# A gated recurrence inside a decoder layer: chunks of 32 tokens against chunks of 64, with operands laid by head and token

## The chip, the cores and the metric

One core of one Trainium2 chip runs the whole program. The metric is device time in microseconds (us) of one execution; the kernel before has a median of 2337.99 us over 3 runs (2333.99 to 2338.67). Engines are called as in the profile: PE (TensorE matmuls), PEld (its weight loads), DVE (VectorE), ACT (ScalarE), POOL (GpSimd), SP (SyncE, which only issues transfers).

## The reference

One layer on x of 2048 tokens by 1024, float32: a norm, an input projection, a token mixer, an output projection, a residual, and then a gated MLP with a convolution. The change concerns the token mixer's recurrence, 8 heads of 64:

```python
def step(state, inp):                       # one token, per head
    r_t, w_t, k_t, v_t, a_t, b_t = inp
    sa = jnp.einsum('bhvk,bhk->bhv', state, a_t)
    state = (state * w_t[:, :, None, :] + sa[..., None] * b_t[:, :, None, :]
             + v_t[..., None] * k_t[:, :, None, :])
    y_t = jnp.einsum('bhvk,bhk->bhv', state, r_t)
    return state, y_t
...
y = rwkv7_recurrence(r_h, hs(decay), k_mod, v_h, -kk, kk * alpha_h)
mean = jnp.mean(y, axis=-1, keepdims=True)
var = jnp.mean(jnp.square(y - mean), axis=-1, keepdims=True)
y = (y - mean) * lax.rsqrt(var + GN_EPS) * ln_x_w + ln_x_b      # by head
return (y + bonus) * g
```

Both kernels compute it in chunks: within a chunk the tokens act on one another through a triangular matrix made of products of b and a, whose inverse is applied to what comes from the state and from v (giving u), and the state then takes b times u plus k times v. The inverses of 32 by 32 blocks are found on DVE, row by row.

## The kernel before

Three parts follow one another. `phase_project` (0 to about 541 us) does the norm and the input projection in 4 blocks of 512 tokens, makes r, k, v, a, b and the decays, and stores them to DRAM. `phase_recur` (548 to about 860 us) runs the recurrence. `mix_out_programs` and `phase_out_and_ffn` do the rest. In the projection and the MLP nearly every product is split in three (`split_matmul`, L133 to L135).

In `phase_project` the names that matter are `rows` (it turns a block of features by tokens into tokens by features on PE, L899), called for v and for a (`dec`), and `a_rows`, `store_rows` and `store`, with which ACT copies and stores them; `gram` (L915) makes the products of b and a of which DVE later inverts the 32 by 32 blocks (`solve` for blocks 0 and 1 of the sequence, in this phase).

`phase_recur` works on tiles of SC = 128 tokens, N = 16 of them, in a software pipeline. `iterations` calls `body(i)` for i from -2 to 19 on each engine. `stages(i)` says what runs: a1 (loads and grams of tile i+2), a2 (preparation of tile i+1), b (state steps of tile i), o (output of tile i-1), c (group norm of tile i-2), d (turning and gating of tile i-3). Every engine has its own program, in the order written, and waits on semaphores with constants. In one steady body PE does, with fp32 operands:

- b: four times, once for each 32-token chunk, `from_state` (4 products, L1673) and `to_state` (8 products, L1681); between them ACT reads u (`read_u`, L1402), and after them DVE updates the state (`advance`, L1553, or L1556 and L1559).
- a2: `bk_transposes` (16 turns of 128x128, L1706), `z0_products` (16, L1729), `w_products` (32, L1747), `z` (16, L1666).
- a1: `grams` (32, L1717), masked by DVE in two instructions (`masks`, L1565).
- o: `from_r` (32, L1694) and `from_uv` (32, L1702). d: the turning of y (4, L1781).

That is 228 products, of which 20 are turns. DVE also does the group norm (L1592 to L1627, six instructions, with the square on ACT) and, in `gap`, the rows of the inverses of blocks 2 and 3 (L1500, L1509, L1511: 27 parts per block, 8 gaps in a body). POOL copies b and k into the zero-padded layout `bk` (L1353, 8 copies in a body) and applies bonus and gate (L1367, L1369). SP issues 18 loads in a body: b, k, a, r, v (4), a by rows (4), the inverses (4, `spread`), bonus and gate.

## Time and profile before

| | |
|---|---|
| median of 3 runs | 2337.99 us |
| span of the profiled execution | 2329.1 us |
| PE busy | 2231.0 us (96%) |
| PEld, DVE, ACT, POOL busy | 78%, 75%, 49%, 44% |
| PE records / weight loads | 16652 / 16652 |
| DMA | 395.6 MB, mean 170 GB/s |

The profiled execution's span goes from its first to its last instruction; no other time of that same execution is given, and the median of the runs is 8.9 us longer than the span. Matmuls are pipelined and their ends are modelled: a PE that reads as busy may be waiting between two starts. So in the stretches of small products the starts and the counts of the records are read here, not the busy time. A plain fp32 product is two MATMUL records and two LDWEIGHTS records; a turn (transpose) is one of each.

### The profile page before, as it was taken

The page shows a single profiled execution, that of the slowest core. Times are in us where ns is not written, and L with a number is a line of the kernel's source. Part 1 is how long each engine was busy: PE and PEld are TensorE (multiplying, and loading weights), DVE is VectorE, ACT ScalarE, POOL GpSimd, SP SyncE. Part 2 cuts the span into 40 slices and gives each one's busy share as a digit, 9 for nine tenths or more (in the row PEclk, how much of TensorE's full clock was granted, in tenths as well). Part 3 has the DMA queues.
Part 4 walks back from the last instruction along what each step waited for, and adds up shares of the span by engine and source line. Part 5 has one row for each costly group of instructions (what it writes and reads, how often), then busy time and mean ns, then how long its engine had stood idle before and what let it go on. Part 6 is the DMA issues. An engine that isn't in the chain of part 4 may idle for free.

```text
span 2329.1 us, 43634 instructions
## 1 busy us (share of the span) xinstructions
PE 2231.0 (96%) x16652; PEld 1816.6 (78%) x16652; DVE 1756.5 (75%) x1910; ACT 1141.8 (49%) x1795; POOL 1025.4 (44%) x726
## 2 busy tenths in 40 slices
PE   7999999996999979998999999999999999999998
PEld 6777777775878768887888888788788888887886
DVE  3756798994884466769989999666799898976565
ACT  5646556452445554444444444454554444444543
POOL 4636466571234335535776766100146555541000
PEclk9999999998999989999999999999999999999999
DMA  7364556347567547895434343677733332326774
GB/s 203 93 227 134 178 160 209 106 140 216 154 166 194 144 144 234 268 279 166 153 119 147 121 146 128 217 252 255 237 119 115 104 111 93 113 95 202 247 260 145
DMA packets 435819, 395.61 MB, mean 170 GB/s; under 512 B 59548, under 2 KB 352076, under 8 KB 432332
## 3 DMA queue, kind: packets, MB, share of 16 engines
q1 hardware_dynamic: 407804, 343.06, 47.8%
q10 hardware_dynamic: 27856, 50.34, 6.0%
q8 instruction: 111, 1.82, 0.3%
q14 instruction: 48, 0.39, 0.1%
HBM read 266.97 MB, written 126.35 MB: 169 GB/s over the span
## 4 chain that ended last, share of the span: by engine, by line
PE 55%; DVE 3%; DMA 2%; ACT 1%; issue 1%; SPq 0%; ACTq 0%; POOLq 0%; POOL 0%; DVEq 0%
PE late_bank L133 18%; PE late_bank L134 18%; PE late_bank L135 18%; DVE wt_lo L2906 1%; DMA scratch_a<-p_keep 1%; ACT wt_hi L2727 1%; PE late_bank L2199 1%; DMA o_lo<-scratch_q 0%; DVE wt_lo L2860 0%; DMA p_keep<-in_w_down 0%; DMA raw<-in_w_down 0%; DMA scratch_x<-x_tile 0%; DMA p_keep<-scratch_td 0%; DVE p_ub L2869 0%; DVE x_tile L2168 0%
## 5 line engine op out<-in xcount | busy, mean ns | idle before, releaser
L133 PE MATMUL late_bank<-o_hi,wt_hi 128*128 128x512 f32 x1232 | 481.3, 391 | 8.0 <-DVE o_lo L2962 3.3
L134 PE MATMUL late_bank<-o_lo,wt_hi 128*128 128x512 f32 x1232 | 480.7, 390 | 0.0
L135 PE MATMUL late_bank<-o_hi,wt_lo 128*128 128x512 f32 x1232 | 480.6, 390 | 0.0
L431 POOL TENSOR_TENSOR p_w_lo<-p_w_raw,p_w_hi 128x1024 fp32r<-128x1024 f32 x72 | 190.4, 2645 | 221.2 <-ACT p_w_hi L502 221.2
L133 PEld LDWEIGHTS late_bank<-o_hi,wt_hi 128*128 128x128 f32 x1232 | 232.0, 188 | 58.7 <-issue 7.2
L135 PEld LDWEIGHTS late_bank<-o_hi,wt_lo 128*128 128x128 f32 x1232 | 232.1, 188 | 48.8
L134 PEld LDWEIGHTS late_bank<-o_lo,wt_hi 128*128 128x128 f32 x1232 | 232.0, 188 | 47.8
L2597 POOL TENSOR_TENSOR tsum<-raw 128x512 f32<-128x512 f32 x43 | 106.2, 2469 | 358.5 <-DVE p_ub L2947 179.4
L133 PE MATMUL p_ppr<-p_hT_hi,p_w_hi 128*128 128x512 f32 x576 | 233.4, 405 | 0.2 <-ACT p_ring L513 0.2
L133 PE MATMUL late_bank<-wt_hi 128*128 128x512 f32 x572 | 223.2, 390 | 7.2 <-DVE wt_lo L2906 6.6
L135 PE MATMUL p_ppr<-p_hT_hi,p_w_lo 128*128 128x512 f32 x576 | 226.6, 393 | 0.0
L134 PE MATMUL p_ppr<-p_hT_lo,p_w_hi 128*128 128x512 f32 x576 | 226.5, 393 | 0.0
L135 PE MATMUL late_bank<-wt_hi,wt_lo 128*128 128x512 f32 x572 | 222.6, 389 | 0.0
L134 PE MATMUL late_bank<-wt_lo,wt_hi 128*128 128x512 f32 x572 | 222.6, 389 | 0.0
L2674 ACT ACTIVATE wt_hi<-tsum 128x512 fp32r<-128x512 f32 x172 | 107.4, 627 | 169.3 <-PE late_bank L135 165.2
L2906 DVE TENSOR_TENSOR wt_lo<-raw,wt_hi 128x1024 fp32r<-128x1024 f32 x96 | 121.3, 1265 | 90.9 <-ACT wt_hi L2727 90.5
L2869 DVE TENSOR_TENSOR p_ub<-late_bank,p_ub 128x512 f32<-128x512 f32 x220 | 150.2, 683 | 34.6 <-PE late_bank L135 33.3
L2860 DVE TENSOR_TENSOR wt_lo<-raw,wt_hi 128x512 fp32r<-128x512 f32 x130 | 153.5, 1181 | 28.8 <-ACT wt_hi L2674 28.7
L2727 ACT ACTIVATE wt_hi<-raw 128x1024 fp32r<-128x1024 f32 x96 | 101.6, 1061 | 116.0 <-PE late_bank L135 96.9
L2860 DVE TENSOR_TENSOR wt_lo<-tsum,wt_hi 128x512 fp32r<-128x512 f32 x173 | 153.3, 887 | 1.8 <-ACT wt_hi L2674 0.6
L133 PEld LDWEIGHTS p_ppr<-p_hT_hi,p_w_hi 128*128 128x128 f32 x576 | 109.2, 190 | 36.3 <-issue 12.7
L133 PEld LDWEIGHTS late_bank<-wt_hi 128*128 128x128 f32 x572 | 107.4, 188 | 32.4 <-issue 6.4
(328 smaller groups left out, 4679.3 us busy)
## 6 DMA issues: line engine op xcount, KB each, us to landing
raw<-in_w_up SPq DMA_DIRECT2D x88, 512.0 KB, 5.1
p_w_raw<-in_w_in SPq DMA_DIRECT2D x72, 512.0 KB, 3.9
scratch_a<-p_keep SPq DMA_DIRECT2D x22, 1280.0 KB, 4.5
raw<-scratch_a SPq DMA_DIRECT2D x96, 256.0 KB, 3.0
raw<-scratch_td SPq DMA_DIRECT2D x52, 256.0 KB, 3.7
p_keep<-scratch_a SPq DMA_DIRECT2D x47, 256.0 KB, 2.9
scratch_a<-p_keep SPq DMA_DIRECT2D x44, 256.0 KB, 2.0
raw<-in_w_down SPq DMA_DIRECT2D x44, 256.0 KB, 4.1
```

The source lines that it names most:

```text
L133: nc.tensor.matmul(out, lhs_hi, rhs_hi, start=start, stop=False, skip_group_check=again)
L134: nc.tensor.matmul(out, lhs_hi, rhs_lo, start=False, stop=False, skip_group_check=again)
L135: return nc.tensor.matmul(out, lhs_lo, rhs_hi, start=False, stop=stop, skip_group_check=again)
L431: nc.gpsimd.tensor_tensor(w_lo[i][:, :, :], w_raw[i][:, :, :], w_hi[i][:, :, :].bitcast(F32), ALU.subtract).then_inc(s_wl, 1)
L2199: last = nc.tensor.transpose(bank[:, 4 + 2 * p + k // 4, (k % 4) * P:(k % 4 + 1) * P], hx[p][:, k * P:(k + 1) * P], ident[:, :])
L2597: nc.gpsimd.tensor_tensor(T1, B12, B11, ALU.subtract).then_inc(s_t, 1)
L2674: nc.scalar.activation(wt_hi[:, ph, :, :], weights(p, ph), ACT.Copy).then_inc(s_uh, 1)
L2727: nc.scalar.activation(dn_hi[r], dn_raw[r], ACT.Copy).then_inc(s_dh, 1)
L2860: nc.vector.tensor_tensor(wt_lo[:, ph, :, :], weights(p, ph), wt_hi[:, ph, :, :].bitcast(F32), ALU.subtract).then_inc(s_ul, 1)
L2869: nc.vector.tensor_tensor(dst, bank[:, b, :], src, ALU.add).then_inc(s_cd, 1)
L2906: nc.vector.tensor_tensor(dn_lo[r], dn_raw[r], dn_hi[r].bitcast(F32), ALU.subtract).then_inc(s_dl, 1)
```

## The change

The recurrence now works on chunks of L = 64 tokens. The tile of 128 tokens has two chunks and eight heads, and all operands lie with head h of a pair on partitions 64h to 64h+63, or with the tokens of a chunk there. A product takes 64 partitions and gives 64; `half(h)` to `half(h)` or `half(h)` to `other(h)`. In most loops two kinds of product alternate, so that four successive products name the four different 64x64 corners of the array:

```diff
+                    def from_state(c2):
+                        pe.wait_ge(s_z, ONE + i + 1)
...
+                        for j in range(PAIRS):
+                            for h in range(2):
+                                own = nc.tensor.matmul(pbank[half(h), c2 * PAIRS + j, :], ar[now][half(h), j, 0, tokens(c2)],
+                                                       st[p][c2][half(h), j, :], start=False, stop=True, skip_group_check=True)
+                                kv = nc.tensor.matmul(sbank[half(h), j, :], bkt[p][other(h), 1, (c2 * PAIRS + j) * H:(c2 * PAIRS + j + 1) * H],
+                                                      uv[now][other(h), 1, c2 * PAIRS + j, :], start=j == 0, stop=False, skip_group_check=True)
...
+                    def inverse(j, h, c2):
+                        u = c2 * PAIRS + j
+                        return nc.tensor.matmul(ubank[half(h), u, :], xt[now][half(h), j * 2 + c2, :], pz[half(h), u, :],
+                                                start=True, stop=True, skip_group_check=True)
```

The PE body before and after, in the order of the program (the number of products of the body after is in the table below):

```diff
-                        from_state(0)
...
-                        bk_transposes(0)
...
-                        to_state(0)
...
-                        from_r(0)
...
+                    if b:
+                        from_state(0)
+                    if o or a2:
+                        from_r_and_gram_of_a()
+                    if b or o:
+                        inverse_first()
+                    if a2:
+                        corner()
+                    if d:
+                        turn_y()
+                    if b or o:
+                        to_state_first()
+                    if o:
+                        from_u()
+                    if b:
+                        from_state(1)
+                    if a2:
+                        corner_right()
+                    if b or a2:
+                        inverse_second()
+                    if a2:
+                        gram_of_b_and_turn_k()
+                    if b or a2:
+                        to_state_second()
+                    if a2:
+                        turn_b_and_z()
+                        corner_left(0)
+                        corner_left(1)
```

| loop after | products | kinds, corners |
|---|---|---|
| from_state (0), (1) | 2 x 16 | state times a, and k times v: four corners |
| from_r_and_gram_of_a | 32 | r times state, and a with k: four |
| inverse_first, to_state_first | 2 x 16 | inverse or b times u, and v into y: four |
| inverse_second, to_state_second | 2 x 16 | inverse or b times u, and r with k: four |
| gram_of_b_and_turn_k, turn_b_and_z | 2 x 32 | r with b and turned k; turned b and z: four |
| turn_y, from_u | 2 x 16 | one kind: two corners |
| corner, corner_right, corner_left (0), (1) | 16, 16, 8, 8 | 32 wide: they make the lower block of the 64x64 inverse from the two 32x32 ones |

The sum is 272. Turning is done with plain products by the identity, no longer with `transpose`. `corner_left(1)` waits for `corner_left(0)` to be complete. The other engines:

```diff
-                        act.wait_ge(s_p1, ONE + i * CH + c4 + 1)
-                        nc.scalar.activation(uv[slot - 1][urows(e), c4, :, :], ubank[p][urows(e), c4 // 2, :, :], ACT.Copy).then_inc(s_u, 1)
...
+                        act.wait_ge(s_as, ONE + i * 2 + c2 + 1)
+                        nc.scalar.activation(pz[:, four(c2), :], pbank[:, four(c2), :], ACT.Copy).then_inc(s_p, 1)
...
+                        act.wait_ge(s_xp, ONE + i * 2 + c2 + 1)
+                        nc.scalar.activation(uv[i % BATCH][:, 0, four(c2), :], ubank[:, four(c2), :], ACT.Copy).then_inc(s_u, 1)
...
+                GAPS = 6
+                TURNS = 5
...
+                        nc.gpsimd.tensor_tensor(y[n % 3][:, :, :], y[n % 3][:, :, :], stat[p][:, 0, :].unsqueeze(2).to_broadcast([P, HEADS, H]),
+                                                ALU.add).then_inc(s_yc, 1)
...
+                        nc.gpsimd.tensor_tensor(y2[:, :, :], y[n % 3][:, :, :], y[n % 3][:, :, :], ALU.mult).then_inc(s_sq, 1)
...
+                        nc.gpsimd.tensor_tensor(y[n % 3][:, :, :], y[n % 3][:, :, :], stat[p][:, 3, :].unsqueeze(2).to_broadcast([P, HEADS, H]),
+                                                ALU.mult).then_inc(s_yc2, 1)
```

POOL no longer copies b and k; it takes over centring, squaring and scaling of y (three instructions of 128x512), and keeps bonus and gate. DVE masks three grams of 128x512 instead of two of 128x1024, updates the state twice with two instructions each instead of four times with one or two, and gets a 32x32 block transpose of 128x128. The rows of the inverses are spread over 5 bodies of 6 gaps. ACT reads p and u twice each, l21, m1, turned k, turned b, y and the corner x21.

In `phase_project` `a_rows`, its turns on PE and its stores go; the stores of a, r, b, k, bonus and gate go to arrays laid (block, partition, pair, tile, kind, token) in pieces of 128 tokens. SP loads two kinds in one transfer: b with k, a with r, bonus with gate; v in 2 transfers; the inverses in 12 (4 into `xt`, 8 into `xd`). That is 17 loads in a body. At the start of the recurrence the five parameter loads are the first of SP, and body -2 has no PE work.

## Rows read from the trace of the kernel before

**Rows 1.** Busy time of the page, and of bodies 0 to 14 of the recurrence (PE, PEld, DVE, ACT, POOL, clock, DMA share, GB/s).

```profile
PE 2231.0 (96%) x16652; PEld 1816.6 (78%) x16652; DVE 1756.5 (75%) x1910; ACT 1141.8 (49%) x1795; POOL 1025.4 (44%) x726
...
579.99:814.18 234.19, 220.10 (x6100) 190.24 (x6096) 156.19 (x306) 117.07 (x270) 78.14 (x132) 0.99 0.60 165
```

**Rows 2.** Timeline of PE in one body: start, us, line, product, records.

```profile
617.04 0.68 PE L1673 MATMUL late_bank<-p_st,p_w 128*64 128x64 f32 x8
617.65 0.66 PE L1706 MATMUL late_bank<-p_ident,first_bk 128*128 128x128 f32 x4
618.24 0.69 PE L1681 MATMUL late_bank<-p_uv,p_bkt 128*64 128x64 f32 x16
618.85 0.65 PE L1694 MATMUL late_bank<-p_st,p_ar 64*32 64x64 f32 x32
619.43 0.66 PE L1781 MATMUL late_bank<-p_ident,p_y 128*128 128x128 f32 x4
...
621.21 0.69 PE L1681 MATMUL late_bank<-p_uv,p_bkt 128*64 128x64 f32 x16
...
625.84 1.15 PE L1729 MATMUL late_bank<-p_uv,am 64*64 64x64 f32 x32
...
632.46 0.68 PE L1673 MATMUL late_bank<-p_st,w 128*64 128x64 f32 x8
```

**Rows 3.** Groups of PE: products of 512 columns on 64 and on 128 rows; turns of a.

```profile
L892 PE MATMUL p_pm<-p_um,p_wlora 64*128 64x512 f32 x64 | 15.9, 615 | 0.0
L884 PE MATMUL p_pm<-p_um,p_wgate 128*128 128x512 f32 x32 | 14.4, 592 | 0.0
...
L899 PE MATMUL p_pm<-p_ident,p_dec 128*128 128x128 f32 x48 | 5.7, 272 | 0.0
```

**Rows 4.** Windows between starts after stalls, columns as in the second of rows 1.

```profile
781.15:804.70 23.55, 21.66 (x635) 18.96 (x635) 10.38 (x19) 11.98 (x28) 5.54 (x10) 1.00 0.52 148
...
698.20:703.05 4.85, 3.88 (x126) 3.48 (x127) 1.66 (x4) 3.11 (x8) 2.54 (x2) 1.00 1.00 287
717.46:721.45 3.99, 3.73 (x137) 3.41 (x129) 2.88 (x5) 1.51 (x4) 3.41 (x8) 1.00 0.60 163
...
801.01:804.70 3.69, 3.49 (x136) 3.18 (x133) 2.34 (x5) 2.00 (x5) 0.00 (x0) 1.00 0.22 66
```

**Rows 5.** DMA queues from 781.1 to 804.7 us and from 580 to 815 us.

```profile
q8 instruction: 5, 0.08, 1.2%
...
q8 instruction: 48, 0.79, 1.4%
```

**Rows 6.** PE starts after idle time with no releaser; then such waits in the projection.

```profile
703.07 1.39 PE L1717 MATMUL late_bank<-ar,bk 128*64 128x64 f32 x40 [0.95 <-issue]
...
PE p_pm L915 <- issue: 8.5, 4, 2.8
```

**Rows 7.** Timelines of ACT and DVE in that body: reading u, updating the state.

```profile
617.76 0.38 ACT L1402 ACTIVATE p_uv<-late_bank 64x256 f32<-64x256 f32 x1 [1.22 <-PE late_bank L1673]
...
622.01 0.42 DVE L1556 TENSOR_TENSOR p_sumst<-late_bank,p_st 128x256 f32<-128x256 f32 x1 [0.39 <-PE late_bank L1681]
622.48 0.43 DVE L1559 TENSOR_TENSOR p_st<-p_sumst,chunk_decay 128x256 f32<-128x256 f32 x1
622.93 0.69 DVE L1592 TENSOR_REDUCE p_stat<-p_y 128x8 f32<-128x512 f32 x1
```

**Rows 8.** Groups of DVE in the recurrence: rows of the inverses.

```profile
L1511 DVE TENSOR_TENSOR p_inv<-p_inv,p_prod 128x30 f32<-128x30 f32 (+14 forms) x60 | 25.1, 419 | 2.1
L1509 DVE TENSOR_TENSOR p_prod<-p_inv 128x30 f32<-128x30 f32 (+14 forms) x60 | 23.7, 396 | 0.9
```

**Rows 9.** Timelines of DVE and of POOL at the same moment.

```profile
624.97 0.19 DVE L1509 TENSOR_TENSOR p_prod<-p_inv 128x30 f32<-128x30 f32 x1
625.20 1.30 DVE L1511 TENSOR_TENSOR p_inv<-p_inv,p_prod 128x30 f32<-128x30 f32 x1
...
625.17 1.28 POOL L1367 TENSOR_TENSOR p_mo<-p_mo,p_bonus 128x512 f32<-128x512 f32 x1 [11.96 <-DMA p_gate<-scratch_g]
```

**Rows 10.** Window with the clock at half, and PE's timeline there.

```profile
642.30:649.10 6.80, 6.80 (x119) 6.06 (x119) 3.91 (x6) 3.35 (x8) 3.81 (x6) 0.50 0.81 229
...
643.96 1.08 PE L1694 MATMUL late_bank<-p_st,p_ar 64*32 64x64 f32 x32
```

**Rows 11.** Timelines: ACT at the projection's end, PE at the recurrence's start and end.

```profile
542.43 1.27 ACT L556 ACTIVATE p_gate<-p_pm,p_par 128x512 f32<-128x512 f32 x2 [0.44 <-ACT p_cum L595]
...
557.18 1.11 PE L1706 MATMUL late_bank<-p_ident,first_bk 128*128 128x128 f32 x4 [4.01 <-DMA p_lnb<-in_ln_x_b]
...
819.83 0.68 PE L1673 MATMUL late_bank<-p_st,p_w 128*64 128x64 f32 x8 [0.57 <-ACT p_w L1392]
...
832.13 1.08 PE L1694 MATMUL late_bank<-p_st,p_ar 64*32 64x64 f32 x32 [0.86 <-ACT p_y L1472]
```

More of the change, by code:

```diff
@@ L37 @@
 CH = SC // C
+L = 2 * C
+HEADS = 2 * PAIRS
 UNITS = PAIRS * CH
@@ L652, in _ @@
                             high_w(n + WB)
-                        if f == 1 and b > 0:
-                            a_rows(b - 1, [pm[:, g, :] for g in range(TT)])
                         if f == 2:
@@ L929, in small @@
                 def small(b, pair):
-                    if pair == 0 and b > 0:
-                        pe.wait_ge(s_abr, ONE + b)
-                        rows(dec, [pm[:, g, :] for g in range(TT)], s_atn)
                     if pair in (2, 3) and b > 0:
@@ L1188, in job @@
             for other in JOBS[:JOBS.index(name)]:
-                if TURN[other] == t and (d if other[0] == "y" else a2):
+                if TURN[other] == t and (d if other == "y" else a2):
                     before += 1
@@ L1284, in body @@
+                        for h in range(2):
+                            sp.dma_start(uv[n % BATCH][other(h), 1, :, :].rearrange("s (c j) v -> s c (j v)", c=2), vrow[n, h]).then_inc(s_v[n % 2], 16)
+                        if n == 1:
+                            load_ab(FIRST)
+                            sp.dma_start(above[:, :, :], const_view(a, "above")).then_inc(s_ab, 16)
                     if N - 2 - KT <= i < N - 2:
@@ L1473, in body @@
                     if a2:
[L1474 to L1480 removed]
+                        take("x21", *((xt[(i + 1) % BATCH][quad(h, 0), :, C:L].rearrange("s (j c) t -> s c j t", c=2),
+                                       lambda v, h=h: v[quad(h, 0), 0:HEADS * C].rearrange("p (c j t) -> p c j t", c=2, t=C)) for h in range(2)))
@@ new lines, in to_state, with r_of_k @@
+                    def to_state(j, h, c2):
+                        u = c2 * PAIRS + j
+                        return nc.tensor.matmul(sbank[half(h), j, :], bkt[p][half(h), 0, u * H:(u + 1) * H], uv[now][half(h), 0, u, :],
+                                                start=False, stop=True, skip_group_check=True)
+                    def r_of_k(j, h, c2):
+                        return nc.tensor.matmul(units(KB)[other(h), c2 * PAIRS + j, :], kinds[half(h), j, 1, tokens(c2)],
+                                                ar[nxt][half(h), j, 1, tokens(c2)], start=True, stop=True)
@@ L1687, in from_r @@
-                    def from_r(h2):
-                        if h2 == 0:
-                            pe.wait_ge(s_yr, ONE + i - 1)
-                        else:
-                            pe.wait_ge(s_yh, ONE + i)
-                        for j in range(PAIRS):
-                            for c4 in range(CH):
-                                last = nc.tensor.matmul(ybank[C * c4:C * c4 + C, j * 2 + h2, :], old[half(h2), 1, j, c4 * C:c4 * C + C],
-                                                        st[q][c4][half(h2), j, :], start=h2 + j == 0, stop=True, skip_group_check=True)
-                        last.then_inc(s_yd if h2 else s_yh, 1)
@@ new lines, in from_r_and_gram_of_a, with from_u @@
+                        if o:
+                            own.then_inc(s_yd, 1)
+                        if a2:
+                            ak.then_inc(s_gd, 1)
+                    def from_u():
+                        pe.wait_ge(s_yd, ONE + 3 * (i - 1) + 2)
+                        for c2 in range(2):
+                            for j in range(PAIRS):
+                                for h in range(2):
+                                    u = c2 * PAIRS + j
+                                    last = nc.tensor.matmul(ybank[half(h), u, :], ark[(i - 1) % 3][half(h), 0, c2, j, :], uv[old][half(h), 0, u, :],
+                                                            start=False, stop=True, skip_group_check=True)
+                        last.then_inc(s_yd, 1)
@@ new lines, in turn_y @@
+                    def turn_y():
+                        pe.wait_ge(s_yc2, ONE + i - 2)
+                        at, full = place_of("y")
+                        for j in range(PAIRS):
+                            for c2 in range(2):
+                                for h in range(2):
+                                    last = nc.tensor.matmul(at[half(h), j * SC + c2 * L:j * SC + c2 * L + L],
+                                                            y[(i - 3) % 3][half(h), c2 * PAIRS + j, :], ident[half(h), half(h)], start=True, stop=True)
+                        last.then_inc(full, 1)
```

825 lines of the change are left out of this document (382 added, 443 removed).

## The prediction

> **What bounds the kernel now.** I read the page first: PE is busy for 96% of the span, every other engine for less [rows 1]. So only what shortens PE's path, or adds a wait to it, can move the time. The MLP and the output projection are not touched. What is left is the recurrence, 548 to 860 us, and a few products of the projection.
>
> In the recurrence I read the starts in PE's timeline. A body, from one from_state(0) to the next, takes 632.46 - 617.04 = 15.42 us [rows 2]. From the z0 products of body 0 to those of body 14 there are 234.19 us and 6100 records [rows 1], at 436 in a body (2 x 208 + 20) 14 steps of 16.73 us. PE has no large wait for another engine in these steps. Why is the mean 1.3 us longer than a smooth body? Counting answers that. Between two starts that follow a stall, 781.15 and 804.70 us, PE has 635 products and 635 weight loads [rows 4]; with the six or so bare semaphore instructions of a body that is 1280, or 5 times 256, and the instruction queue q8 moved 5 packets meanwhile [rows 5]. Between 698.20 and 703.05 us it is 126 + 127, again one 256 [rows 4], and the idle 0.95 us at the end of it has no releaser, only "issue" [rows 6]. So PE's program comes in blocks of 256 instructions, one DMA packet each, and PE stands still where the next block is not there. From 580 to 815 us it needed 48 blocks [rows 5], one in 4.9 us. The densest loop of the projection, L915, shows the same stall at its worst: 8.5 us in 4 waits, up to 2.8 us [rows 6].
>
> How fast can blocks come? Three steps that ended in such a stall took 4.85, 3.99 and 3.69 us, with the DMA engines 100%, 60% and 22% taken [rows 4]. The next block is evidently asked for only when the one before is entered, or these steps would have been shorter. Stalled blocks are a biased choice, the late ones among 48; in the changed kernel early ones count too. I take 3.85 us, near the lower end, with 3.5 and 4.2 us as bounds of the mean.
>
> The Trainium skill, "Runtime: NRT & Kernel Launch", section "Instruction fetch mechanics", says that instructions are refilled in blocks of 256 by a DMA queue of the sequencer's own, and calls the cost of a boundary "mostly hidden". The counts above agree with the block size. That it is hidden is what rival 1 assumes.
>
> **The change, part by part.**
>
> *PE's arithmetic.* A loop of 16 products on two corners (L1729, 32 records) takes 1.15 us. One of 16 products on four column strips (L1694, 32 records) takes 619.43 - 618.85 = 0.58 us [rows 2]. Do two products that share columns but not rows also run side by side? L892 has 64 records of 64 rows in 15.9 us, L884 32 records of 128 rows in 14.4 us [rows 3]: twice the products in nearly the same time, so they do. The 272 products after are 17 groups of 16, of which two (turn_y, from_u) use two corners: 15 x 0.58 + 2 x 1.15 = 11.0 us against 15.4. PE's arithmetic falls by 4.4 us in a body.
>
> *PE's program.* 228 products, 20 of them single turns, are 2 x (208 x 2 + 20) = 872 instructions; 272 plain products are 1088. With some ten for waits: 1098 / 256 = 4.29 blocks against 3.43. At 3.85 us that is 16.5 us a body; at 3.5 it is 15.0, at 4.2 it is 18.0. This is more than 11.0, so the blocks bound PE, not the products. Against 16.73 us: -0.2 us a body, for 14 steps **-3.0 us** (-24 to +18).
>
> *The chain through the engines.* From the start of from_state to ACT's read is 617.76 - 617.04 = 0.72 us, the read 0.38, and the next product starts at 618.24: 1.20 us [rows 2, 7]. The chunk of 64 has two such links, and one to DVE: 622.01 - 621.21 = 0.80 us from the start of to_state to L1556, then 0.42, 0.43 and some 0.15 for the gaps [rows 2, 7]. That is 1.2 + 1.2 + 1.8 = 4.2 us, 8.4 for both chunks, under other products of PE for most of it. It costs nothing while 16.5 us stand; without that cover it is part of rival 1.
>
> *DVE, ACT, POOL.* DVE's own work after: the masks as three of 0.69, the value of the reduction of the same size, state 4 x 0.43, two reductions 1.38, and some 0.6 of small things [rows 7], 5.8 us. The inverses cost 48.8 us in all [rows 8], over 9 bodies 5.4. Together 11.2 us, below 16.5. POOL has five instructions of 1.28 us [rows 9], 6.4. ACT has about 6.5 by the durations of its reads. None of them is the bound by itself. The lock between DVE and POOL is in rival 3.
>
> *Loads.* One transfer fewer in a body, and fewer pieces, though larger; the eight extra of the inverses are small. At a body of 16 us the DMA share stays near the 0.60 of [rows 1], so I leave 3.85 as it is. SP's queue has about 9 us of issuing, with waits on work that is one body old: hidden, and at an 11 us body nearly not.
>
> *The projection.* The turns of a go: 48 in the path of three blocks, 5.7 us of PE [rows 3], **-5.7 us**, since PE's next product waits for nothing else there. The stores in pieces of 128 tokens only load DMA and ACT's queue, not PE; bounds 0 to +3. At its end the last pool products reach ACT at 542.43 us after the rows of a [rows 11]; without them about 1 us sooner: **-1.0 us** (0 to -3).
>
> *Start of the recurrence.* PE waited until 557.18 us for the last parameter load [rows 11], which after is issued before the tile loads, some 2.4 us sooner. Then PE waits for the inverses, whose 12 transfers take about 6 us to issue. I take **-2.0 us** (-5 to +3).
>
> *The bodies without preparation.* Body 15 took 832.13 - 819.83 = 12.3 us up to the second from_r [rows 11]. After, its 136 or so products are 2.1 blocks or 8.2 us, about the chain's 8.4, with ACT's copies of the output weights between: **-3.0 us** (-5 to +2). The y of the last tile passes POOL three times more, behind dense products.
>
> Sum: -3.0 - 5.7 - 1.0 - 2.0 - 3.0 = -14.7 us on a span of 2329.1, so 2314.4; with the 8.9 us that the median lies above the span, **2323.3 us**.
>
> **The rivals.**
>
> 1. *The blocks come in time.* Then PE is bound by 11.0 us of products and the chain, about 11.5 us in 5 steps, and in the 9 with inverses by DVE, 11.2 us plus half of POOL's 6.4, some 14: 9 x 14 + 5 x 11.5 = 183.5 against 234.2, -50.7 - 11.7 gives 2275.6 us. Against it: stalls stand exactly at multiples of 256 already at 872 instructions in 15.42 us, 57 per us, and 1098 in 11 us are 100 per us.
>
> 2. *The clock falls (slower).* After the idle time around 639 us PE ran at the 1.2 GHz level from 642.30 to 649.10 us, granted clock 0.50, and a from_r that takes 0.65 us took 1.08 [rows 2, 10]. After, PE computes for 11.0 of 16.5 us, with a stall in every block. At that level 11.0 becomes 11.0 x 1.08/0.65 = 18.3 us, with the chain some 19: 14 x (19 - 16.73) = +31.8, less 11.7, gives +20, 2358 us. It makes the change slower once over half of the bodies run so. Against it: the 0.95 us stall [rows 6] left the clock at 1.00 [rows 4].
>
> 3. *DVE and POOL lock each other on top of it.* A DVE instruction of 0.19 us took 1.30 while POOL's ran, and ended with it [rows 9]. If none of POOL's 6.4 us lies beside free DVE time, a body with inverses is 11.2 + 6.4 = 17.6 us: 9 x 17.6 + 5 x 16.5 = 240.9, +6.7 - 11.7, 2333 us. The Trainium skill, "SBUF — State Buffer", says that the port pair of the two is an exclusive lock, for DVE instructions with two SBUF inputs against POOL's; the row agrees.
>
> 4. *The four corners don't overlap*, so the change does not do what it says. PE's arithmetic is then 17 x 1.15 = 19.6 us less the short loops, about 17.5: 14 x 0.8 = +11, -11.7, 2337 us. Rows 3 speak against it. The Trainium skill, "TensorEngine Tiling (Array Packing)", section "Restrictions and Gotchas", says that different row tiles can't use one PSUM bank at a time; L1729 has both its corners in one bank, and its 1.15 us for 16 [rows 2] shows no such halt.
>
> **How the numbers follow.** Chances: forecast (3.5 to 4.2 us a block) 0.55, rival 1 0.15, rival 2 0.15, rival 3 0.10, rival 4 0.05. The forecast alone runs from 2302 to 2344. The range takes in rival 1's 2275 and stops short of rival 2's end: 2275 to 2350. A difference under 0.2%, 4.7 us, can't be told from none by measurements of this kernel. Faster by more: 0.47 of the forecast's 0.55, all of rival 1, 0.03 each of rivals 3 and 4: 0.68. Within: 0.05 + 0.01 + 0.04 + 0.01 = 0.11. Slower: 0.03 + 0.14 + 0.03 + 0.01 = 0.21.
>
> **What would show it.** PE's products in bodies 0 to 14 start in bursts, with idle time put down to "issue" once in 256 instructions and q8 packets 3.5 to 4.2 us apart; a body takes 15 to 18 us though its records fill only 11; 16 products on four corners take 0.6 us; DVE has time left in bodies 10 to 14. The projection's blocks are 1.9 us shorter from the second on. It is wrong if q8 packets come under 3 us apart (rival 1), if the granted clock of 580 to 815 us is under 0.9 (rival 2), or if PE's waits in bodies 0 to 8 are put down to DVE's state (rival 3).

## The result and the profile after

The changed kernel is slower: 2394.91 us median (2390.94 to 2397.45) against 2335.99 us, ratio 1.0257, 95% interval 1.0235 to 1.0280. The forecast was 2323 us, its range ended at 2350. The profiled execution has a span of 2392.9 us, 63.8 more than before's 2329.1.

The page's busy times of the kernel after, against [rows 1]: PE is busy 35 us less, although the span is 64 us longer. So PE waits some 100 us more.

```profile
PE 2196.0 (92%) x18316; PEld 1792.0 (75%) x18316; DVE 1731.4 (72%) x1875; ACT 1097.4 (46%) x1715; POOL 1013.4 (42%) x645
```

Where? Four marks in PE's timeline divide the run: the end of its last projection product, from_state(0) of body 0 and of body 15, the first output product. Before (columns as in [rows 2]; body 15 is in [rows 11]):

```profile
539.71 1.88 PE L926 MATMUL p_pm<-p_kk,p_wpool 128*128 128x512 f32 x4
...
568.37 0.68 PE L1673 MATMUL late_bank<-p_st,w 128*64 128x64 f32 x8
...
838.00 0.50 PE L133 MATMUL late_bank<-w_hi,m_hi 128*128 128x512 f32 x1 [0.92 <-DVE m_lo L1605]
923.19 0.39 PE L133 MATMUL late_bank<-w_hi,m_hi 128*128 128x512 f32 x1
```

After:

```profile
555.86 3.75 PE L906 MATMUL p_pm<-p_kk,p_wpool 128*128 128x512 f32 x4 [1.45 <-ACT p_gate L547]
...
581.55 0.27 PE L1586 MATMUL late_bank<-p_st,first_ar 64*64 64x64 f32 x1
...
875.39 0.27 PE L1586 MATMUL late_bank<-p_st,p_ar 64*64 64x64 f32 x1
...
892.06 0.50 PE L133 MATMUL late_bank<-w_hi,m_hi 128*128 128x512 f32 x1
986.31 0.39 PE L133 MATMUL late_bank<-w_hi,m_hi 128*128 128x512 f32 x1
```

The last line of each is the 101st product of L133 of the output. The differences:

| stage | before | after | change | forecast |
|---|---|---|---|---|
| projection, to PE's last product | 541.59 | 559.61 | +18.0 | -6.7 |
| on to body 0 | 26.78 | 21.94 | -4.8 | -2.0 |
| bodies 0 to 14 | 251.46 | 293.84 | +42.4 | -3.0 |
| body 15 to the output | 18.17 | 16.67 | -1.5 | -3.0 |
| first 100 products of L133 | 85.19 | 94.25 | +9.1 | 0 |
| rest | 1405.9 | 1406.6 | +0.7 | 0 |

*The bodies.* Windows over the 15 bodies, before and then after (columns as in [rows 1]):

```profile
568.40:819.80 251.40, 232.28 (x6338) 200.49 (x6336) 164.47 (x322) 123.69 (x284) 80.13 (x136) 0.98 0.60 163
```

```profile
581.55:875.39 293.84, 199.13 (x7974) 181.33 (x7969) 145.99 (x295) 89.42 (x226) 71.16 (x62) 0.80 0.49 138
```

PE's products fill 33 us less, at a granted clock of 0.80 instead of 0.98. Its waits without a releaser ("issue") go from 5.0 us in 9 waits to 79.9 us in 41, summed over the lines of the view of waits. The largest, the wait of body 0 for DVE's state, and one in the timeline:

```profile
PE late_bank L1600 <- issue: 9.7, 4, 3.1
PE late_bank L1769 <- issue: 9.5, 5, 3.6
PE late_bank L1783 <- issue: 8.6, 3, 4.0
PE late_bank L1757 <- issue: 7.1, 4, 2.5
...
PE late_bank L1586 <- DVE p_st L1478: 5.7, 1, 5.7
```

```profile
707.98 0.36 PE L1771 MATMUL late_bank<-p_ident,bk 64*64 64x64 f32 x1 [3.57 <-issue]
```

The queue of PE's program brought 64 blocks there, one in 293.8 / 64 = 4.6 us:

```profile
q8 instruction: 64, 1.05, 1.4%
```

The stalls stand at the ends of blocks. Between two starts that follow such a wait PE has about 253 records (products and weight loads; with the bare semaphore instructions a block of 256), or twice or three times that, in all 40 steps between the 41 waits. A step of one block and one of two:

```profile
701.65:707.98 6.33, 2.67 (x126) 2.35 (x127) 3.95 (x6) 1.05 (x3) 2.34 (x2) 0.86 0.56 183
720.61:730.78 10.17, 7.33 (x253) 6.82 (x254) 5.10 (x9) 3.64 (x9) 2.59 (x2) 0.67 0.47 140
```

Body 14 has the same program as body 13, but SP has no tiles or weights left to load. It is 7 us shorter, its DMA share 0.08 instead of 0.65 (body 13, then 14):

```profile
838.99:860.63 21.64, 14.63 (x547) 13.24 (x544) 5.48 (x13) 6.22 (x16) 5.52 (x6) 0.74 0.65 186
860.63:875.39 14.76, 11.97 (x548) 10.98 (x545) 4.99 (x11) 6.22 (x16) 5.65 (x5) 0.91 0.08 23
```

*The projection.* The group L915, which waited 8.5 us for "issue" [rows 6], waits 0.9 us after (L895 there). A wait of another kind is new: PE at turn_x, for DVE's part of the turned x. In the view of waits it is 5.9 us in 4 before, and after:

```profile
PE p_ptr L956 <- DVE p_hT_lo L693: 26.6, 4, 9.2
```

PE's timeline, then ACT's queue ahead of it, show why:

```profile
144.72 1.11 PE L956 MATMUL p_ptr<-p_ident,x_block 128*128 128x128 f32 x4 [8.26 <-DVE p_hT_lo L693]
...
129.73 1.32 ACTq L514 DMA_DIRECT2D scratch_bg<-p_tmp  x1
131.10 6.17 ACTq L514 DMA_DIRECT2D scratch_bk<-p_alpha  x1
...
137.66 3.81 ACTq L514 DMA_DIRECT2D scratch_ar<-p_dec  x1
```

The same two issues took 1.42 and 1.20 us before. ACT stands in them, copies the next turned x late, DVE follows, PE waits 8.26 us, and then works at half clock for some us (the products of L133 to L135 start 0.43 us apart instead of 0.23).

*The output.* Turning y for the last two tiles waits for POOL, which after the change also scales y and here has output weights to prepare too; before, one wait of 1.9 us, for DVE's y, stood there.

```profile
900.31 1.59 PE L1757 MATMUL late_bank<-p_ident,p_y 64*64 64x64 f32 x32 [3.88 <-POOL p_y L1317]
...
910.31 1.39 PE L1757 MATMUL late_bank<-p_ident,p_y 64*64 64x64 f32 x32 [3.00 <-POOL p_y L1317]
```

### The profile page after: what moved, and what is told of

Same layout as the page of the kernel before. It is cut to its first block, busy times and chain, and to the rows that moved or that the text cites. A ratio compares the mean times of both kernels' runs of the same rounds, so it can differ in the third digit from the quotient of the medians.

```text
span 2392.9 us, 46822 instructions
## 1 busy us (share of the span) xinstructions
PE 2196.0 (92%) x18316; PEld 1792.0 (75%) x18316; DVE 1731.4 (72%) x1875; ACT 1097.4 (46%) x1715; POOL 1013.4 (42%) x645
## 4 chain that ended last, share of the span: by engine, by line
PE 53%; DVE 3%; DMA 3%; ACT 1%; issue 1%; SPq 0%; ACTq 0%; POOLq 0%; POOL 0%; DVEq 0%
PE late_bank L133 18%; PE late_bank L135 17%; PE late_bank L134 17%; DMA scratch_a<-p_keep 1%; DMA raw<-in_w_down 1%; DVE wt_lo L2926 1%; ACT wt_hi L2747 1%; PE late_bank L2219 0%; DMA scratch_x<-x_tile 0%; DMA o_lo<-scratch_q 0%; DMA raw<-scratch_td 0%; DVE wt_lo L2880 0%; DMA raw<-in_w_up 0%; DVE x_tile L2188 0%; DVE p_ub L2889 0%
## 5 line engine op out<-in xcount | busy, mean ns | idle before, releaser
L133 PE MATMUL late_bank<-o_hi,wt_hi 128*128 128x512 f32 x1232 | 481.7, 391 | 9.0 <-DVE o_lo L2982 3.3
L135 PE MATMUL late_bank<-o_hi,wt_lo 128*128 128x512 f32 x1232 | 480.3, 390 | 0.0
L133 PEld LDWEIGHTS late_bank<-o_hi,wt_hi 128*128 128x128 f32 x1232 | 232.0, 188 | 60.1 <-issue 8.5
L135 PEld LDWEIGHTS late_bank<-o_hi,wt_lo 128*128 128x128 f32 x1232 | 231.9, 188 | 48.5
L133 PE MATMUL p_ppr<-p_hT_hi,p_w_hi 128*128 128x512 f32 x576 | 233.6, 406 | 2.5 <-ACT p_ring L504 2.1
L133 PE MATMUL late_bank<-wt_hi 128*128 128x512 f32 x572 | 223.3, 390 | 6.4 <-DVE wt_lo L2926 5.9
L135 PE MATMUL p_ppr<-p_hT_hi,p_w_lo 128*128 128x512 f32 x576 | 226.6, 393 | 0.0
L135 PE MATMUL late_bank<-wt_hi,wt_lo 128*128 128x512 f32 x572 | 222.6, 389 | 0.0
L133 PEld LDWEIGHTS p_ppr<-p_hT_hi,p_w_hi 128*128 128x128 f32 x576 | 109.1, 189 | 40.3 <-issue 16.8
L133 PEld LDWEIGHTS late_bank<-wt_hi 128*128 128x128 f32 x572 | 107.3, 188 | 32.1 <-issue 6.6
```

The costliest lines, as they stand in the source:

```text
L133: nc.tensor.matmul(out, lhs_hi, rhs_hi, start=start, stop=False, skip_group_check=again)
L135: return nc.tensor.matmul(out, lhs_lo, rhs_hi, start=False, stop=stop, skip_group_check=again)
```

## The experiments

### The layout in DRAM

```diff
-            return scr[key][b][:, :, :, m, :].rearrange("p j g t -> p (j g) t")
+            return scr[key][b][:, :, m, :, :].rearrange("p j g t -> p j (g t)")
...
-    scr = {k: scratch(k, (BLOCKS, P, PAIRS, TT, 2, SC)) for k in ("ar", "bg", "bk")}
+    scr = {k: scratch(k, (BLOCKS, P, PAIRS, 2, TT, SC)) for k in ("ar", "bg", "bk")}
```

> The kernel after with one change: the arrays of a and r, b and k, bonus and gate lie in DRAM as (block, partition, pair, kind, tile, token), so that the projection stores them in pieces of 512 tokens (2 KB) as the kernel before did, and the recurrence loads them in pieces of 512 B. Theory: the stores in pieces of 128 tokens hold ACT's queue (issues of 6.17 and 3.81 us, L514), so ACT turns x late and PE waits 8.26 us at L956. Then the two issues fall to about 1.4 and 1.2 us, that wait goes, PE's last product of the projection ends 18 to 25 us sooner (559.6 to about 536 to 541 us), and the time falls from 2395 to 2370 to 2377 us. Rival: the projection is longer for another reason (half clock after the grams, stalls of PE's program); then the time stays within 5 us of 2395. The recurrence's bodies should stay at 19.6 us, at most 20 with the smaller pieces.

Measured: 2373.67 us, ratio 1.0191 (1.0156 to 1.0225); the kernel before, run beside it, had a median of 2328.66 us, so by the ratios the gain is 15 us, by the medians 21. In the profiled execution the span is 24.9 us shorter. PE's projection ends at 528.27 + 1.95 = 530.22 us, 29 us sooner than after (more than the 18 to 25 expected) and 11 sooner than before, and the issues are short again:

```profile
130.09 1.43 ACTq L514 DMA_DIRECT2D scratch_bk<-p_alpha  x1
...
131.91 1.30 ACTq L514 DMA_DIRECT2D scratch_ar<-p_dec  x1
...
528.27 1.95 PE L906 MATMUL p_pm<-p_kk,p_wpool 128*128 128x512 f32 x4 [1.45 <-ACT p_gate L547]
```

The waits at turn_x are 5.9 us in 4 again, as in the kernel before. The 15 bodies take 293.0 us, as after. The store theory is shown, and the forecast's direction for the projection was right where the stores don't stand in ACT's way.

### Loads thinned

```diff
-                            sp.dma_start(rows(ar[n % BATCH]), group("ar", n)).then_inc(s_in[n % 2], 16)
+                            one = slice(0, 1 if n >= BATCH else P)
+                            sp.dma_start(rows(ar[n % BATCH])[one], group("ar", n)[one]).then_inc(s_in[n % 2], 16)
```

(and the same for b and k, v, bonus and gate, the inverses)

> The kernel after, but from tile 4 on every load of the recurrence (b and k, a and r, v, bonus and gate, the inverses) moves only the first partition of what it moved, so the output isn't the reference's; instructions and waits are the same. If transfers delay the fetch of PE's blocks (DMA share 0.49 in bodies 4 to 14), blocks come 3.7 us apart or less, those bodies fall from 20 to 15.5 to 16.5 us, the granted clock rises to 0.95, and the time falls by 35 to 45 us to about 2355. If the fetch alone has this latency and order, the bodies stay at 19 to 20 us and the time within 8 us of 2395.

Measured: 2360.22 us in one run. Bodies 4 to 14 in this kernel, then in the kernel after:

```profile
656.10:842.60 186.50, 133.48 (x5988) 119.67 (x5985) 108.20 (x207) 68.27 (x176) 62.55 (x55) 0.92 0.20 61
```

```profile
654.10:875.40 221.30, 153.04 (x5993) 139.64 (x5987) 104.84 (x206) 68.49 (x176) 63.33 (x55) 0.78 0.50 142
```

Both have 47 blocks there: one in 3.97 us instead of 4.71. A body takes 16.95 us instead of 20.1: 3.2 us hang on the transfers, close to what was expected. Of the 34.8 us, the waits for "issue" make 61.5 - 45.2 = 16.3 and PE's busy time, for the same products at a higher clock, 19.6. That is a count and not what a full clock would give back: a PE that works faster waits longer for the same block, and no run here has the one without the other. What the run shows is that both shrink when the transfers go.

### Many small products, or few large ones, in the kernel before

```diff
+                        for n in range(14):
+                            q4 = slice(C * (n % 4), C * (n % 4) + C)
+                            nc.tensor.matmul(bank[q4, SB, 0:1], ident[q4, q4], ident[q4, 0:1], start=True, stop=True)
```

> The kernel before with 14 products of one column put ahead of the products of each to_state, written where those write next: 56 in a body, 224 instructions, so that a body has 1096 or so, as after. If PE's program is the bound at the price that the kernel after shows (64 blocks in 293 us, 4.58 us each), a body takes 4.28 x 4.58 = 19.6 us against 16.76, 15 bodies +42 us, 2338 becomes 2380. If the products and the chain are, 56 small products add 1.7 us by the 0.036 us of one of L1694's, of which 0.3 to 1.7 show in a body: +5 to +25 us.

```diff
+                        nc.tensor.matmul(bank[:, SB, 0:PAIRS * H], ident[:, :], ident[:, :].unsqueeze(1).to_broadcast([P, 2, P]), start=True, stop=True)
```

> The kernel before with one product of 128x128 by 256 columns ahead of the products of each to_state, written where those write next: 4 in a body, 16 instructions, some 1.8 us of PE. By the program's price that is 0.06 of a block, 0.3 us; what the arithmetic costs shows: 15.4 + 1.8 = 17.2 us of PE against a body of 16.76, so +0.4 to +1.8 us a body, +7 to +27 us in all. If the many small ones cost much more than this, it is their number that costs.

Measured: 2364.62 us, ratio 1.0138 (1.0103 to 1.0173), with the many; 2354.59 us, 1.0106 (1.0073 to 1.0140), with the few. The bodies, many and then few:

```profile
570.20:854.10 283.90, 257.02 (x8021) 223.34 (x8017) 163.06 (x322) 123.89 (x284) 81.27 (x136) 0.98 0.53 145
```

```profile
564.80:840.80 276.00, 264.69 (x6460) 216.15 (x6456) 165.91 (x322) 124.00 (x284) 80.83 (x136) 0.99 0.55 149
```

Read by PE's own time: 14 small ones take 0.35 us (the next product starts 0.35 us after the first of them), 1.4 in a body, and the body grows by 18.93 - 16.76 = 2.2. The large ones take 0.62 each, 2.5 in a body, and it grows by 1.6. "Issue" makes 16.2 us with the many, 2.3 with the few. In the medians the many cost 36 us, between the two sums that were stated (42, and 5 to 25), and the few 26, at the upper end of 7 to 27. So the number costs beyond the arithmetic, but a body of 1096 instructions does not take the expected 19.6 us: 64 blocks come 4.4 us apart, at a clock of 0.98. A fixed price of a block is a poor model.

### PE kept busy in the kernel after

```diff
+                            for _ in range(2):
+                                nc.tensor.matmul(bank[:, ROT[t], TB // 2:TB], ident[:, :], ident[:, :].unsqueeze(1).to_broadcast([P, 2, P]),
+                                                 start=True, stop=True)
```

> The kernel after with two products of 128x128 by 256 columns ahead of each of six loops that write a turning bank (corner, corner_right, corner_left(0), turn_y, turned k, turned b): 12 in a body, 48 instructions, each 0.62 us of PE by the same product in the run with few added (L1679), 7.4 us in all. They change no result. They fill time in which PE stood still, and should keep its clock up. If the low clock is what makes a body 19.6 us instead of 16.5, the granted clock rises from 0.84 to 0.95 or more and bodies take 17 to 19 us. If the supply of the program is the bound, the clock rises too, but a body takes (1098 + 48) / 256 x 4.6 = 20.6 us, 19.8 to 21.5, +3 to +28 us in all. If neither holds and PE's work simply adds up, a body takes up to 27 us, +110.

Measured: 2425.84 us, ratio 1.0396. Its 15 bodies, 21.4 us each:

```profile
583.80:904.20 320.40, 265.52 (x8327) 212.69 (x8321) 149.37 (x298) 89.02 (x226) 71.96 (x63) 0.94 0.45 127
```

That is 31 us more than after, just above the 3 to 28 of the supply theory; the body is in its range. The clock rises to 0.94 and "issue" halves to 39.9 us, but the added 7.4 us a body cost more than both give back. This does not clear the clock: PE's busy time is 17.7 us a body, so it would hardly have fallen below that.

### Half the instructions

```diff
+            return v.bitcast(mybir.dt.bfloat16)[:, 1::2]
```

(on both operands of every product of the recurrence)

> The kernel after, but in the recurrence every product reads only the upper 16 bits of its operands, as bf16, in one pass instead of two: the same products, waits and transfers with half the instructions (some 554 in a body, 2.16 blocks), and coarser numbers, so the output isn't the reference's. If the supply of the program is the bound, a body needs 2.16 x 4.6 = 9.9 us of it, and what is next shows: the chain of 8.4 us and DVE's 11.2. Bodies with inverses 11.5 to 14 us, the others 9.5 to 11.5, 15 bodies 110 to 140 us less, the time about 2265 to 2285. If DVE and POOL locking each other is what holds the bodies, those with inverses stay over 17 us. If the low clock is, the clock falls further with PE less busy and the bodies stay over 16.

Measured: 2305.21 us in one run. Window of the bodies, and the largest waits from 560 to 860 us:

```profile
582.80:784.00 201.20, 91.50 (x3999) 74.36 (x3994) 145.39 (x297) 83.85 (x227) 67.62 (x60) 0.50 0.71 197
...
PE late_bank L1175 <- DVE p_st L1484: 51.7, 17, 8.8
PE late_bank L1175 <- issue: 34.1, 20, 4.0
PE late_bank L1175 <- POOL p_y L1323: 10.7, 6, 3.8
```

13.4 us a body, 93 us less in all; I had expected 110 to 140. One pass instead of two halves PE's arithmetic with its instructions, so this run alone does not part the two. It does part them from the clock: the clock is at half throughout, and still the bodies are short. Waits for DVE's state now lead: bodies 2 to 9, with inverses, take 14.3 us, and DVE is busy for 63.9 of 72.9 us in five of them; bodies 10 to 13 take 12.9. So DVE is the next bound, at 14 us and not at the 17 that the lock would have made.

### The grams of the projection spread

```diff
-                        if b > 0 and 1 <= k <= TT:
-                            gram(b - 1, (k - 1,))
+                        if b > 0 and 1 <= k <= 2 * TT:
+                            gram(b - 1, ((k - 1) // 2,), range((k - 1) % 2 * 2, (k - 1) % 2 * 2 + 2))
```

> The kernel before with the grams of a projection block spread over 8 steps of the next block's first pair, 16 products in a step, instead of over 4 steps with 32 (and ACT's read of them after its last turned x). Same instructions, less dense: 84 instead of 148 per step of about 2.4 us. If PE's stalls of 2.64 us and its half clock after them (L915, 8.5 us in 4 waits) come from the supply of the program, they go: three blocks shorter by 3 to 5 us each, 2338 falls by 8 to 15 us. Rival: the stalls only move to where the next block ends; then within 3 us of no change.

Measured: 2330.98 us against 2331.53, ratio 0.9997 (0.9985 to 1.0009), where 8 to 15 us less was expected: a miss. The view of waits shows fewer stalls than the 8.5 us in 4 waits of before:

```profile
PE p_pm L915 <- issue: 2.1, 1, 2.1
```

and PE's projection ends at 536.27 instead of 541.59 us. But three other runs here have the projection of before unchanged, and it ends at 537.11, 538.70 and 543.58 us in them, with 4.3, 5.9 and 7.2 us of such waits. So 536.27 is only 0.8 us below the earliest of four executions of the unchanged projection, and a gain is not shown. The bodies, with the same instructions, took 256.9 instead of 251.5 us in the profiled execution. Why is not settled; one execution each can't tell more.

### Fewer instructions at the same work

```diff
+                                        ak = nc.tensor.matmul(bank[other(h), AB + c2, j * 2 * L:(j + 1) * 2 * L], kinds[half(h), j, 1, tokens(c2)],
+                                                              ar[nxt][half(h), j, :, tokens(c2)], start=True, stop=True)
```

> The kernel with the other layout in DRAM (the first experiment), and in it the products of k with a and of k with r made as one, 64 rows by 128 columns, 16 in place of 32, a and r side by side in two banks, masked by DVE in two instructions of 128x512: 64 instructions fewer in a body, 1034 or 4.04 blocks instead of 4.29; inverse_second and to_state_second have 8 products instead of 16. PE's arithmetic stays within 0.5 us. If the number of instructions is the bound at 4.6 us a block, a body takes 18.4 us against 19.53 in that kernel: 15 bodies -12 to -18 us, 2374 becomes 2356 to 2362. If products, chain or clock are the bound, nothing changes: within 5 us of 2374.

```diff
+                                last = nc.tensor.transpose(at[half(0), j * P:(j + 1) * P], kinds[:, j, 1, tokens(c2)], ident[:, :])
```

> The kernel with the merged products (1034 instructions a body), and in it k and b turned by transposes of 128x64 in one pass, 16 of 2 instructions in place of 32 products of 4: 96 instructions fewer, some 938, 3.66 blocks instead of 4.04. The turned blocks come out on 64 partitions, in two banks each, and ACT copies head by head, 8 copies in place of 2 (+1 us of ACT, which has time). If the number of instructions is the bound at 4.6 to 4.75 us a block, a body falls from 19.2 to 17.1, 15 bodies by 25 to 32 us, 2362 to about 2334. If less of a body depends on the number, as the merge suggested (0.33 us for 64 instructions by the profiles), it is 0.5 us a body, -8 us. If the turns' new order on ACT (tk and tb in four jobs) delays the chain, bodies get longer: +5 to +15 us.

Measured: 2361.84 us, ratio 1.0125 (1.0100 to 1.0149), and 2345.06 us, ratio 1.0070 (1.0043 to 1.0097). Each step makes the kernel faster by about 0.6%, in the median as the first was expected; the second falls between its two sizes. The bodies go 293.0, 288.0, 281.4 us. But 59 blocks in 288.0 us are 4.9 us each: the fewer there are, the dearer one is. PE's records fill 202.3 us of these bodies, against 193.1 with the other layout alone, so part of this is PE's own work.

### Loads paced, and everything together

```diff
+                            sp.wait_ge(s_in[n % 2], ONE + 32 * (n // 2) + 16)
```

> The kernel with the merged products, and in it SP waits for b and k to land before it issues a and r, for these before the inverses and v, and for v before bonus and gate. Bytes and pieces are the same, but no long row of transfers stands ahead of a block's fetch. With the loads thinned a body was 3.2 us shorter; if that was the waiting of fetches behind queued loads, pacing gets part of it back: a body 0.5 to 1.5 us shorter, -8 to -22 us, 2340 to 2354. If it was the share of the engines that the bytes take, nothing changes (within 4 us). If SP falls behind, PE waits for b and k or a and r (waits for DMA at the start of a body), and the time rises by up to 30 us.

> Layout, merged products, one-pass turns and paced loads together, and for the last two tiles centring, squaring and scaling of y on DVE instead of POOL, against PE's waits of 3.9 and 3.0 us for POOL's y in the output's first products (L1757). These two go to 1.9 us or less as in the kernel before, -4 to -7 us. With -8 to -28 us by the turns and 0 to -22 by pacing, from 2362: 2305 to 2350, 2334 as the likeliest, level with the kernel before.

Measured: 2403.09 us, ratio 1.0324, and 2401.45 us, ratio 1.0297: both misses. SP's queue became the bound. In it, a body's loads are issued one after the other and wait:

```profile
645.96 0.67 SPq L1230 DMA_DIRECT2D first_bk<-scratch_bk  x1
651.67 0.52 SPq L1234 DMA_DIRECT2D ar<-scratch_ar  x1
655.72 0.31 SPq L1199 DMA_DIRECT2D p_xt<-scratch_inv  x1
...
667.34 0.54 SPq L1260 DMA_DIRECT2D p_bg<-scratch_bg  x1
```

That is 21.4 us from b and k to bonus and gate, over the length of a body, and PE waits for a and r (15.3 us in 7 waits at L1596 alone). The larger wait goes by way of DVE: the inverses' pieces come late, DVE stands at the block transpose of them, which its program has ahead of the update of the state, and PE waits for the state. DVE's and PE's largest waits from 550 to 900 us:

```profile
DVE x1u L1512 <- DMA xd<-scratch_inv: 139.9, 15, 15.4
```

```profile
PE late_bank L1596 <- DVE p_st L1483: 62.9, 15, 15.5
```

The expectation had this case, SP falling behind, at up to 30 us; it was 41. Whether pacing helps where SP keeps up stays untested. The last tiles' part of the run with everything together did what it should: the first 100 output products take 994.59 - 909.18 = 85.4 us, as before.

### What is left: cover or price

> The kernel before with the loads of the recurrence thinned in the same way: from tile 4 on only the first partition of each, so the output isn't the reference's. If a late fetch costs only what PE's products don't cover, there is little to gain here: bodies 4 to 14 go from 16.6 us to the 15.4 of the smooth body, 15.3 to 16.0, -7 to -15 us. If each block has a price that transfers raise by 0.75 us (3.2 us for 4.29 blocks), a body falls by 2.6 us to 14.1.

> The kernel with merged products and one-pass turns (938 instructions, 3.66 blocks), loads thinned in the same way, so the output isn't the reference's. At the 3.95 us a block that the kernel after had with thinned loads a body takes 14.5 us; with the 3.45 of a fetch that nothing delays, 12.6. If the chain or ACT is what holds this kernel at 18.8 us, and not the supply, the bodies stay over 17.

> Layout, merged products and one-pass turns of k and b as before, without pacing, and besides: y turned by 8 one-pass transposes of 128x64 in place of 16 products (48 instructions fewer, 890 or 3.48 blocks a body); centring, squaring and scaling of y for the last two tiles on DVE; and in body 0 DVE's first rows of the inverses after the state's update instead of ahead of it (PE waited 7.9 us for DVE's state there). From 2345: -7 for the last tiles (85.4 against 92.4 us in the run with all together), -5 for body 0, -3 to -10 for the turns of y: 2323 to 2333, against 2330 of the kernel before. If ACT, which gets 8 small reads of y in place of 4, is in the chain's way, up to +10.

Measured: 2322.74 and 2316.11 us, one run each, for the kernel before and the one with one-pass turns. Bodies 8 to 12 of the kernel before, thinned, and the five of the same products in the kernel before:

```profile
698.90:776.10 77.20, 76.77 (x2183) 66.83 (x2181) 42.68 (x71) 43.20 (x100) 33.09 (x53) 1.00 0.20 57
```

```profile
705.50:787.90 82.40, 78.26 (x2183) 67.52 (x2181) 41.16 (x71) 42.98 (x100) 32.26 (x54) 1.00 0.69 185
```

15.4 us a body instead of 16.5, with 17 blocks in both, and no wait for "issue" left. In these five, before's bodies go down to its arithmetic and no further: it is not a price of the block, by which a body was to fall to 14.1. Over all of bodies 4 to 14 the gain is smaller: 182.5 against 187.4 us, 16.6 against 17.0 a body, where 15.3 to 16.0 had been expected. The waits for "issue" go there too (4.5 us before), but five waits for DVE's state (5.8 us; before has three, 3.5 us) stand in bodies 5 to 7, and the clock was 0.84 in body 6 and 0.91 in body 13. The kernel with one-pass turns, thinned and not thinned:

```profile
623.20:796.00 172.80, 155.28 (x5107) 132.24 (x5104) 101.50 (x206) 89.41 (x242) 62.40 (x56) 1.00 0.22 65
```

```profile
627.20:835.70 208.50, 170.88 (x5108) 146.41 (x5104) 102.00 (x206) 89.40 (x242) 63.59 (x56) 0.90 0.56 151
```

15.7 against 18.95 us a body: again 3.2 us, 15.6 of the 35.7 as PE's busy time at a lower clock. The 15.7 is above the 14.5 expected, and most of that is PE's own work: at full clock its records fill 155.28 / 11 = 14.1 us of a body. The one-pass turns take all 128 rows and save no time:

```profile
696.09 0.63 PE L1773 MATMUL late_bank<-p_ident,bk 128*64 128x128 f32 x4
696.64 0.68 PE L1778 MATMUL late_bank<-ar,bk 64*64 64x64 f32 x16
697.25 0.63 PE L1773 MATMUL late_bank<-p_ident,bk 128*64 128x128 f32 x4
```

Four turns take 0.55 us and the eight products behind them 0.61, four times in a body, 4.6 us, where the 64 products that stood there (both turns, r with b, and z) were forecast at 4 x 0.58 = 2.3. So fewer instructions were bought with more arithmetic, and these kernels do not vary the number alone.

The kernel with all that had helped gave 2348.71 us, ratio 1.0085 (1.0063 to 1.0108), where 2323 to 2333 was expected: a miss, and not faster than the 2345.06 without the last three steps. The last tiles gained 4.8 us and body 0 1.6, but the turns of y with ACT's 8 small reads brought nothing (280.4 us for 15 bodies, against 281.4), body 15 took 2.9 us more up to the output, and PE's projection, which has the same program in both, ended 3 us later. No version here that does the whole work beats the kernel before.

## Why the prediction was wrong

The span was forecast at 2314.4 us and came out at 2392.9. Of the 78.5 us between them the bodies have 45.4, the projection 24.7, the first output products 9.1.

*What bounds the kernel.* Right: PE's program in blocks of 256 bounded the bodies after, and the idle time stood where it was said to stand, as "issue", at the ends of blocks.

*3.85 us a block: the step that failed.* It was 4.6 us (64 blocks in 293.8). The three steps of [rows 4] gave 4.85, 3.99 and 3.69 us at DMA shares of 100, 60 and 22%, and I took a value near the lower end, as if stalled blocks were the late ones and the rest would pull the mean down. In the kernel before, products cover 4.5 us of each block (15.4 / 3.43), so that most late fetches leave no trace in it. After, they cover 2.6 (11.0 / 4.29), so that nearly all do, and after a stall products run at half clock. The thinned runs show it: nearly without transfers a body of after takes 16.95 us, close to the 16.5 forecast; with them 20.1; body 14, with hardly any, takes 14.8. For the kernel before the same step is 1.0 us in five bodies (82.4 against 77.2) and 0.4 over eleven. How a transfer makes a fetch late, by a queue ahead of it or by the engines' share, is not shown. The share was even lower than the forecast left it, 0.49 and not 0.60, and "At a body of 16 us the DMA share stays near the 0.60 of [rows 1], so I leave 3.85 as it is" was the sentence to doubt: the step of 3.99 us at 60% was already above 3.85.

*PE's arithmetic, 11.0 us.* As costed: in the last full body from_state, four corners, starts at 867.92 us and the next loop at 868.54 us, 0.62 against 0.58; from_u, two corners, takes 0.97 against 1.15. Rival 4 is out.

*The clock, rival 2.* It asked for a granted clock under 0.9, and this came: 0.80 over the bodies. Its mechanism was right in direction and I dismissed it on one stall of 0.95 us; the longest stalls are 2.5 to 4.6 us here. But it is no rival: it came with the stalls and shrank with them, and of the 34.8 us that the transfers cost bodies 4 to 14 longer products are 19.6. Its own share is not shown: with the clock back at 0.94 by added products the bodies were no shorter. The price given, 19 us a body with half clock throughout, was reached at 0.80.

*Rival 3.* Out: bodies 10 to 13, without inverses, take 21.6 us in the mean, those with inverses 19.3. In one of 23 us DVE is busy for 5.6 and POOL for 5.7:

```profile
815.00:838.00 23.00, 15.17 (x546) 14.02 (x544) 5.62 (x12) 6.07 (x17) 5.67 (x5) 0.72 0.46 128
```

*Rival 1.* Out: it asked for blocks under 3 us apart, and they came 4.6 us apart.

*The projection, -6.7 us.* With the stores put back in longer pieces it ends 11.4 us sooner than before. That is more than the 6.7, but 6.5 of it are waits for "issue" in the grams (8.5 us before, 2.0 there), which the forecast did not count and which vary from run to run; what is left fits the turns of a. "Only load DMA and ACT's queue, not PE" failed: the queue of ACT is in PE's path at the start of each block, through the turned x, and the bound of +3 us was set with no row on how an issue's time grows with its pieces. It cost 29 us of the projection.

*Start and body 15.* -4.8 and -1.5 us against -2.0 and -3.0: right in sign and inside their bounds.

*The last tiles.* "Behind dense products" failed: 9 us. In the two runs with DVE in POOL's place these products take 85.4 and 87.6 us, in the others with the new recurrence 91.7 to 94.8. The sum left it out because it named a cover and didn't count POOL's other work there.

*Span and median.* 8.9 us were added for the median above the span; after, it is 2.0. All runs listed lie some 2 us above their own spans, so before's profiled execution took about 2331 us and was faster than the median.

## What to carry to other kernels

Where a loop of small products ends in idle time without a releaser, count its instructions in blocks of 256 and compare a block's arithmetic with the time of a fetch under the transfers that run beside it. Splitting products to use more corners of the array shortens the arithmetic and takes the cover away: here 4.4 us less arithmetic in a body (the forecast's sum) came with 2.8 us more time. And an issue on a compute engine's queue is that engine's time, and here it grew with the number of pieces. A last one: before a gain of some us in one stage is believed, look at how much that stage varies between runs in which its program is the same; here the projection's end varied by 6 us.

## What was not expected of the hardware

- At the end of a projection block an issue of a 1 MB store in 2 KB pieces takes 0.6 to 1.4 us of ACT's queue, in 512 B pieces 1.3 to 6.2 us, while the DMA engines are nearly fully taken.
- Fetches of PE's program come later when loads run: one in 4.71 us at a DMA share of 0.50, one in 3.97 us at 0.20, with the same 47 blocks; 3.7 us in body 14 of the kernel after (4 blocks in 14.8 us, share 0.08). The Trainium skill, "Runtime: NRT & Kernel Launch", section "Instruction fetch mechanics", calls the cost of a boundary "mostly hidden"; in these bodies it was 79.9 us of waits in 293.8.
- In the kernel with half the instructions the granted clock was 0.50 over all 15 bodies, and a body still took 13.4 us.
- Four turns of 128x64 take 0.55 us, as much as 16 products of 64x64 on four corners (0.58 us).
